# Moving the start of every weight ring in SBUF by up to 192 bytes, in a two-block transformer kernel

## What is computed

```python
def mixer(h, hc, lp, rope, n_rows, need_ctx):                      # first block, per layer
    f, nq, nk, nv, cq, ckv, kr, g = jnp.split(h @ lp['w_in'], IN_OFFSETS, axis=-1)
    ...                                                            # Fourier mix, two attentions
    out = merge_branches([y_f, y_na, y_mla], g, lp['w_branch'], lp['w_out'])

def merge_branches(ys, g, w_branch, w_out):
    proj = jnp.einsum('bngi,gio->bngo', jnp.stack(ys, axis=2), w_branch)
    return jnp.sum(jax.nn.sigmoid(g) * proj, axis=2) @ w_out       # shapes left out

def swiglu(h, w_gate, w_up, w_down):
    return (jax.nn.silu(h @ w_gate) * (h @ w_up)) @ w_down

def hybrid_mixer(h, w_in, w_out, ...):                             # second block
    proj = jnp.einsum('bsd,de->bse', h, w_in)
    ...                                                            # window attention, recurrence, attention
    return jnp.einsum('bse,ed->bsd', y, w_out)
```

## Time and profile before

| | us |
|---|---|
| median of 3 runs | 3161.22 (3160.11 to 3162.92) |
| the profiled execution | 3167.77 |
| its span, first to last instruction | 3166.0 |
| PE busy (share of the span) | 2905.9 (92%) |
| PEld busy | 2311.1 (73%) |
| DVE busy | 1687.5 (53%) |
| ACT busy | 1209.3 (38%) |
| mean share of the DMA engines, 40 slices | mostly 0.1 to 0.6 |

### The profile page before, as it was taken

The page is one execution under the profiler, slowest core; times in us unless marked ns, Lnnn a source line. Parts: engine busy times, 40 slices in busy tenths (PEclk is TensorE's granted clock), DMA queues, the critical chain, the costliest instruction groups (busy, mean ns, idle before and its releaser), DMA issues. The chain is left out here.

```text
span 3166.0 us, 37052 instructions
## 1 busy us (share of the span) xinstructions
PE 2905.9 (92%) x14705; PEld 2311.1 (73%) x14705; DVE 1687.5 (53%) x2379; ACT 1209.3 (38%) x1800; POOL 450.9 (14%) x445
## 2 busy tenths in 40 slices
PE   7998899999989999999799799998999978876995
PEld 4886566888868888887587457886888846555774
DVE  3385665233455656643315563446656454655997
ACT  5324555122243212222435443324323244635774
POOL 4400200000030000003400100002000124122332
PEclk9999999999989999999799899999999989887997
DMA  7860101222113444431720103334656335335962
GB/s 207 121 180 19 25 1 50 60 61 70 47 54 108 144 128 127 140 93 41 96 65 16 24 10 100 94 85 119 190 163 190 101 48 74 154 89 183 374 239 80
DMA packets 397871, 330.11 MB, mean 104 GB/s; under 512 B 38038, under 2 KB 340484, under 8 KB 397572
## 3 DMA queue, kind: packets, MB, share of 16 engines
q1 hardware_dynamic: 384196, 304.56, 34.1%
q0 software_dynamic: 13248, 23.13, 3.6%
q10 hardware_dynamic: 256, 0.07, 0.0%
HBM read 331.96 MB, written 30.33 MB: 114 GB/s over the span
## 5 line engine op out<-in xcount | busy, mean ns | idle before, releaser
L1184 PE MATMUL ps<-ahi,w_hi 128*128 128x512 f32 (+1 forms) x2264 | 767.8, 353 | 11.1 <-DVE w_lo L1211 11.1
L1185 PE MATMUL ps<-ahi,w_lo 128*128 128x512 f32 (+1 forms) x2264 | 766.8, 353 | 0.0
L1211 DVE TENSOR_TENSOR w_lo<-w_raw,w_hi 128x1024 fp32r<-128x1024 f32 (+2 forms) x242 | 339.8, 1406 | 373.9 <-ACT w_hi L1201 371.5
L1184 PEld LDWEIGHTS ps<-ahi,w_hi 128*128 128x128 f32 x2264 | 428.0, 189 | 76.7 <-DVE w_lo L1211 14.0
L1187 PE MATMUL ps<-alo,w_hi 128*128 128x512 f32 (+1 forms) x2264 | 473.5, 352 | 0.0
L1185 PEld LDWEIGHTS ps<-ahi,w_lo 128*128 128x128 f32 x2264 | 428.6, 189 | 60.0 <-issue 0.2
L1201 ACT CAST w_hi<-w_raw 128x1024 fp32r<-128x1024 f32 (+2 forms) x244 | 285.5, 1171 | 470.8 <-PE ps L1187 367.6
L1187 PEld LDWEIGHTS ps<-alo,w_hi 128*128 128x128 f32 x2264 | 376.6, 189 | 57.9
L937 DVE SCALAR_TENSOR_TENSOR vec_acc<-vec_w,csilu,vec_acc 128x512 f32<-128x512 f32 x364 | 257.2, 752 | 8.4 <-DVE vec_acc L937 5.7
L1351 POOL TENSOR_TENSOR xsum<-x 128x768 f32<-128x768 f32 (+1 forms) x4 | 6.4, 1592 | 1407.3 <-DVE x L1330 1407.3
L1274 DVE SCALAR_TENSOR_TENSOR x<-ps,mod,x 128x512 f32<-128x512 f32 x80 | 51.4, 668 | 233.7 <-PE ps L1187 220.7
(11 more groups left out here) (556 smaller groups left out, 5185.9 us busy)
## 6 DMA issues: line engine op xcount, KB each, us to landing
vec_w<-in_w_mod SPq DMA_DIRECT2D x128, 512.0 KB, 4.1
w_raw<-in_w_in SPq DMA_DIRECT2D x102, 512.0 KB, 4.3
e_raw<-in_w_gate SPq DMA_DIRECT2D x46, 512.0 KB
e_raw<-in_w_up SPq DMA_DIRECT2D x46, 512.0 KB
e_raw<-in_w_down SPq DMA_DIRECT2D x46, 512.0 KB
w_raw<-in_w_ffn_gate SPq DMA_DIRECT2D x44, 512.0 KB, 4.4
w_raw<-in_w_ffn_up SPq DMA_DIRECT2D x44, 512.0 KB, 4.0
w_raw<-in_w_ffn_down SPq DMA_DIRECT2D x32, 704.0 KB, 4.6
```

Of the source, the lines that this page charges most:

```text
L1184: pe.matmul(o, whi[:, j, b0 + b, :], hi[:, b, t0:t0 + tn], start=(b == 0), stop=False)
L1185: pe.matmul(o, wlo[:, j, b0 + b, :], hi[:, b, t0:t0 + tn], start=False, stop=False)
L1211: dve.tensor_tensor(wlo[:, j, 0:d.blocks, :], raw_of(d, i, jj), whi[:, j, 0:d.blocks, :].bitcast(F32), ALU.subtract).then_inc(lo_ready[j]. ...
```

## The change

`new_ring` puts a small unused tile ahead of the ring, so large that `w_raw` starts at 32 + 128 = 160 modulo 256. The sizes of `w_raw`, `w_hi` and `w_lo` are multiples of 256 bytes in all rings, so all three start at 160, and so does every column block in them (512 bytes each). The moving tiles `ahi`, `alo`, `hhi`, `hlo`, `a2hi` and `a2lo` are allocated ahead of the ring and stay at 32 modulo 256, with rows that are multiples of 256 bytes long. Tiles that are allocated behind a ring, in its own stage, move along by the size of the gap: `yhi`, `ylo`, `sg` and `gp` in rings 2 and 5, and the vector and normalization buffers in ring 1.

```diff
+        def place(ctx, at):
+
+            gap = (at - (nc.sbuf_base + 31) // 32 * 32) % 256
+            if gap:
+                names[0] += 1
+                ctx.enter_context(nc.sbuf_tensor(f"gap_{names[0]}", [P, gap // 4], F32))
...
+        RING_AT = iter([128, 128, 128, 128, 128, 128, 128, 128])
+
         def new_ring(c, blocks):
+            place(c, 32 + next(RING_AT))
             return (sb(c, "w_raw", [P, 2, blocks, P]), sb(c, "w_hi", [P, 2, blocks, P], F32R), sb(c, "w_lo", [P, 2, blocks, P], F32R))
```

## The result

| | before | after |
|---|---|---|
| median, us | 3161.07 | 3184.61 |
| runs | 6, 3157.64 to 3168.99 | 6, 3180.52 to 3189.51 |
| span of the profiled execution, us | 3166.0 | 3183.2 |

The ratio is 1.0071, with a 95% interval of 1.0058 to 1.0085. The forecast was 3157.3 with a range of 3138 to 3183, so the time is outside it, on the slow side.

The account below looks back on a forecast made before the run. The prediction took PE's matmul spacing in the rings as the bound; +1.7, +1.9, -2.4 and -5.1 us summed to -3.9, taking the median 3161.2 to 3157.3 us. The range was 3138 to 3183 us.

Parts of the forecast that it names:

- What bounds the kernel: Inside the rings PE never or hardly pauses, 92% busy overall; time is the number of matmuls times their spacing.
- the split and the landings: DVE's split of the weights (1.26 us) and DMA's landing of weight pieces (4.3 to 4.4 us): hidden by PE, costed at nothing.
- That distance, not stage, sets the spacing: In the rings, weights-to-moving-operand distance modulo 256 sets 512-column spacing: 226.8 ns at 0, 229.1 to 229.4 at 192, 233.4 at 64.
- The counts and the adding up: Matmuls that change distance in the rings, 6240 of 512 and 3072 of 256 columns, times spacing differences; together -3.9 us.
- The `y` matmuls: Matmuls on `yhi` and `ylo` (576 and 288) keep distance 0, as these tiles move with the ring; costed at nothing.
- 128 takes 192's level: All rings at distance 128 get 229.1 to 229.4 ns for 512 columns and 116.6 ns for 256.
- the same -3.9: Forecast sum in us over all rings: +1.7, +1.9 and -2.4 for 512 columns, -5.1 for 256.
- The turn: Mean 512-column spacing at which the change becomes slower: 229.8 ns with 256 columns at 116.6, 0.5 above the forecast's level.
- Between its neighbours: Rival for all rings: distance 128 lies between 192 and 64, 231.3 ns; +9 to +20 us, 3170 to 3181; chance 0.17.
- as bad as 64: Rival: weight load and moving read collide in every ring, 233.4 ns; +33 us, 3194; chance 0.12, including worse.

Follow-up runs that it names:

- The shift by 128 bytes: Kernel before with an unused 128-byte tile ahead of all others, every tile later, no distance changed; ratio 0.9995, 3156.4 against 3159.0 us.
- the shift by 256: Kernel before with 256 unused bytes ahead of rings 1, 3, 4, 6, 7 and 8, distances modulo 256 unchanged; one run, 3155.8 us.
- `alo` against `ylo` in one and the same ring: Changed kernel with rings at distance 0, but 128 unused bytes between `w_hi` and `w_lo`; in ring 5 `w_hi` is 0 from `alo`, 128 from `ylo`; 3177.6 us.
- ring 6 alone: Kernel before with only ring 6 moved from distance 192 to 128; ratio 1.0016 against the kernel before.

## Why the prediction was wrong

- **What bounds the kernel: right.** All of the loss is in the spacing of PE's matmuls in the rings. PE's pauses inside the rings did not grow (in ring 4 they fell by 4 us, which they also do between kernels with the same distances), and costing the split and the landings at nothing held.
- **That distance, not stage, sets the spacing: right, with one exception.** It was read from three levels in the trace of before. The shift by 128 bytes, the shift by 256, the kernels with one distance in all rings, and `alo` against `ylo` in one and the same ring confirm it. The exception is a ring that mixes distances: there the level of a distance isn't always reached (233.1 against 229.6 ns in ring 2 at 192). The Trainium skill, "TensorE: Matmul & The Clock Gate", section "Step-by-step: what each phase is for", says that loading the next weights takes nothing from the running matmul. The traces don't agree with what the prediction took from it, one spacing for all distances: with the same work at the same clock it is 226.8 to 234.3 ns. Which of the two reads gives way, they don't show.
- **The counts and the adding up: right in the main.** With the measured levels the same sum gives +26 us, the medians +23.5; ring 6 alone gave +5.6 by the sum, +5.4 in the trace. The `y` matmuls, costed at nothing, cost 0.4 us in ring 5.
- **The failed step: 128 takes 192's level.** The text gave both bounds, 226.8 to 233.4 ns, and chose 229.1 to 229.4, because two of three known distances were good and "only 64 is far off, which looks like one bad place on the circle". The level at 128 is 232.6 ns, near the upper bound. With it ring 5 costs +4.7 us where +1.9 stood, rings 1, 2 and 4 +7.9 where +1.7 stood, rings 3 and 6 +10.9 where nothing stood, and rings 7 and 8 -0.6 where -2.4 stood. For 256 columns the text had 116.6 ns, and it is 118.7 to 119.5: -0.6 us in rings 1, 2 and 4 where -5.1 stood, and +3.8 in ring 3. The sum was not safe for 192 itself either: with all rings at 192 the time rose by 10 us where the same -3.9 stood, and only part of that is explained.
- **The turn.** "Between its neighbours" (231.3 ns, +9 to +20 us) and "as bad as 64" (233.4 ns, +33) were the rivals that came near; the measured 232.6 ns and +23.5 us lie between them. The turn to slower was put at 229.8 ns, half a nanosecond above the chosen level, and a level known only between 226.8 and 233.4 was given 0.30 for slower and a range that ended at 3183, 11 us short of the bound's own sum. With three known distances of a pattern that need not be smooth, the upper bound belonged in the range.

## What to carry to other kernels

When PE never pauses, look at the distance between the starts of its matmuls and compare stages that do the same thing: a difference of 2 or 3% there is invisible in busy shares and waits and is worth as much as a wait of the same size. For float32r products with 512 moving columns, put weights and moving operand at the same offset modulo 256 bytes; it cost 226.8 ns where most other offsets cost 232 to 234. Here that alone brought no gain clear of no change (0.9993 with all rings at 0), since before most rings were at 0 or 192 already and the 256 columns lose by it; what it avoids is the 21 to 24 us of a bad distance in all rings. A new tile between the moving operand and the weights can shift the offset, so an edit elsewhere can cost this much without touching the product. Measure each offset and each shape, since a neighbour's value tells nothing about the next, and measure rings that mix distances by themselves.

## What the runs showed of the hardware

Mean spacing in ns by the distance of weights from moving operand, modulo 256, with float32r operands, 128 weight columns and the clock at its upper level:

| distance | 0 | 32 | 64 | 96 | 128 | 160 | 192 | 224 |
|---|---|---|---|---|---|---|---|---|
| 512 columns alone (rings 5 to 8) | 226.8 to 227.8 | 233.4 | 233.3 | 234.3 | 232.3 to 232.9 | 233.3 | 229.0 to 229.4 | 233.2 |
| 256 columns (rings 1 to 4) | 119.4 to 119.7 | 118.5 | 113.8 to 115.3 | 117.6 | 118.7 to 119.5 | 119.8 | 115.7 to 117.4 | 116.7 |

The two shapes want different distances: 0 is the best for 512 columns and next to the worst for 256, while 64 is the best for 256 and among the bad ones for 512. Giving the context columns a distance of their own was not tried. The distances 32, 96, 160 and 224 were each seen in one execution alone, for 512 columns in two rings, for 256 in one. Rings that mix distances can be off these levels: ring 2 at 192 took 233.1 ns in its chunks with a `y` part.

The levels are means of uneven steps that repeat: in pairs at 128 in ring 5 of the changed kernel (236.6 and 229.8 ns), in other groups from 228 to 241 ns in its ring 6, and in threes at 192 (231.8, 229.1 and 226.1 ns, ring 6 before). At 0 the steps are even, 226 to 228 ns. At distance 0 the low level is reached only some way behind a run of another shape: in ring 2 before, the first five matmuls behind the 256 columns take 229 to 235 ns in the mean of all chunks, those from the sixth on 226 to 228 (the seven of the earlier trace rows are 231.4 in the mean), and after that it holds.
